# First branch projection of a hybrid decoder layer as four more pairs of seven products, with its token sums made in the mixer

## The chip, the cores and the metric

One core of one Trainium2 chip. The time is that of the device for one execution of the program, in microseconds (us); the median of several runs counts. TensorE (PE) does the matrix products, VectorE (DVE), ScalarE (ACT) and GpSimd (POOL) the elementwise work, SyncE (SP) issues most DMAs. Each engine runs its own instruction stream in order, and the streams meet through semaphores.

## What is computed

One layer of a decoder on 1,024 tokens of width 1,024, float32, from the reference:

```
h = rms_norm(x, norm_w)
proj = einsum('btd,de->bte', h, w_in) + b_in          # 8,720 columns
(a_q, a_k, a_v, a_z, m_q, m_k, m_v, m_i, m_f, m_o, m_z, g_attn, g_mlstm) = split(proj)
attn = sliding_window_sink_attention(a_q, a_k, a_v, sinks)
branch_a = einsum('bte,ed->btd', attn * silu(a_z), w_branch_attn)
h_m = head_rms_norm(mlstm_chunkwise(conv(m_q), conv(m_k), m_v, m_i, m_f))
h_m = sigmoid(m_o) * h_m * silu(m_z)
branch_m = einsum('bte,ed->btd', h_m, w_branch_mlstm)
merged = sigmoid(g_attn) * branch_a + sigmoid(g_mlstm) * branch_m
out = rms_norm(x + einsum('btd,de->bte', merged, w_out), final_norm_w)
```

## The kernel before, in words

**Products.** TensorE multiplies in a format that keeps fewer bits than float32. So each operand is split into a high part (ScalarE, one ACTIVATE Copy) and a low part (full minus high, one TENSOR_TENSOR on VectorE or GpSimd), and a product is the sum of three matmuls: high by high, low tokens by high weights, high tokens by low weights. One matmul takes 128 rows of weights by 512 tokens.

**Pairs.** The input projection is made for two groups of 128 output columns at a time. Such a pair is a 2x2 block product in Strassen's manner: seven products in place of eight, `PRODUCT` = 12 matmuls each (4 slices of 128 features x 3), `PAIR` = 84. The products are called 1, 6, 2, 7, 4, 5, 3, in that order (`ORDER`, L1131), with a bank of PSUM each. Their token operands are seven blocks held in SBUF from the start: `h11`, `s2`, `h12`, `s3`, `h22`, `s1`, `s4`, each a high and a low part of 8 KB per partition, at `H_AT`; three are quarters of the normalised tokens, four are sums of quarters. Their weight operands are four quarters of the pair's weights (`w11`, `w21`, `w12`, `w22`, 256 KB each, loaded by SyncE in `pair_weights`, L617), and three sums made by GpSimd (L818). ScalarE makes the high parts (`high_1` to `high_7`, L1483), GpSimd the low parts (`low`, L820, rows at L823), both in a ring of five slots. VectorE puts the seven banks together (`b_part`, `c11`, `c_part`, `c21`, `c22`, `c12`, L2193 to L2223). A product waits for its weights' low part and for its bank; product 2 of a pair waits for `c12` of the pair before.

**Order of the work.** Turning and norm of the tokens; five dense tiles (k, v, gates); pair 0; four attention steps of three pairs; four mixer steps of five pairs, the last one of four (`WPAIRS` = 32 pairs in all). In an attention or mixer step the small work of the mixer is placed by hand between the matmuls: each of the 8 chunks of a mixer step has two places (`chunk_at`), and on ScalarE and VectorE `retire(position)` (L1783, L2281) does what belongs to the products up to that place. A chunk on TensorE begins with the state products (L1287), which wait for VectorE's state update (L2489 and the operations after it, up to `k_w` at L2517). The gates go to DRAM (`scr_a`, `scr_g`), the attention branch's tokens u to `scr_u`, the mixer's tokens to `scr_m`; those of the last mixer step stay in SBUF (`mz`).

**End of the last mixer step.** TensorE stops 12 matmuls before the end of pair 31, turns the mixer's output (16 transposes, L1315), and does the last 12. Meanwhile SyncE loads u in four blocks of 1 MB over the h blocks as the products of pair 31 end (L670); ScalarE takes a square root with its table load (L1887), then the high parts of u (L1895); VectorE and GpSimd make the low parts.

**Tile stage.** `branch_a_step` (L1362 on TensorE, L1918 on ScalarE, L2566 on VectorE): 8 dense tiles of 48 matmuls (L1344), one per 128 output rows: 8 slices of features x 2 halves of tokens x 3. The weights of a tile (512 KB) are split by GpSimd (`split`, L806 and L808). VectorE multiplies each by its gate into `merged` (L2571) and makes the low parts of the second branch's tokens, held in `UM` at `H_AT` + 64 KB and, for the last two rows, in the mixer's memory (`um_hi67`, `um_lo67`). `branch_m_step` does the same for the second branch and adds (L2619, L2624). Beside it the blocks of the output weights are made: sums s1 to s4 of the quarters (L2596 to L2605), split (L2585), parked in DRAM and loaded back where the memory isn't free yet (`scr_s`, `scr_split`). SyncE's queue is in order: a `wait_ge` in it holds every load behind it.

**End.** Output projection in four pairs of seven products, residual, final norm.

## Time and profile before

| | us |
|---|---|
| median of 3 runs (1077.52 to 1077.68) | 1077.52 |
| the profiled execution | 1077.55 |
| its span | 1075.8 |
| TensorE busy in the span | 1063.5 (99%) |
| VectorE, GpSimd, ScalarE busy | 725.9, 649.7, 516.9 |
| mean granted clock of TensorE, share of full | 0.999 |

The profiled execution is 0.03 us above the median; 1.75 us lie outside its span. A timeline row is start us, us, engine, line, operation, output <- inputs, shape, count, and in brackets the idle time before it and what ended that. Several instructions alike stand in one row ("x2"). Matmuls overlap, so that a matmul's own duration is longer than the distance to the next one.

### The profile page before, as it was taken

To read this page: it belongs to the slowest core of one execution; us is meant where nothing else is said; L and a number is where in the kernel's file an instruction comes from. 1 tells how busy PE (TensorE), PEld (TensorE's weight loads), DVE (VectorE), ACT (ScalarE), POOL (GpSimd) and SP (SyncE) were. 2 spreads that over 40 slices of the span, in tenths; PEclk is the share of its full clock that TensorE was granted. 3 is DMA by queue.
4 is the path that set the end of the run, shared out by engine and by line. 5 is a ranking of instruction groups with operands and counts; after the bars stand their busy time and mean duration, and the time that the engine had idled before them with its cause. 6 is when DMAs were issued, how large, how long until landed. Compare 5 with 4: busy or idle time off the path is not lost.

```text
span 1075.8 us, 18631 instructions
## 1 busy us (share of the span) xinstructions
PE 1063.5 (99%) x6391; PEld 862.7 (80%) x6391; DVE 725.9 (67%) x1144; ACT 516.9 (48%) x1252; POOL 649.7 (60%) x437
## 2 busy tenths in 40 slices
PE   7999999999999999999999999999999999999997
PEld 6887887877877888878888888788788888888886
DVE  5964785776866967566756685669578332558897
ACT  7544755746647643555345444545464311132543
POOL 3577555556555568568955796679654354547441
PEclk9999999999999999999999999999999999999999
DMA  6235132132151231214211431143219434744324
GB/s 220 70 93 89 41 118 80 41 121 76 45 158 40 80 118 40 50 41 147 79 41 50 127 99 39 39 127 88 60 37 363 148 97 151 250 147 164 149 92 143
DMA packets 113851, 111.83 MB, mean 104 GB/s; under 512 B 7340, under 2 KB 96744, under 8 KB 112760
## 3 DMA queue, kind: packets, MB, share of 16 engines
q1 hardware_dynamic: 102648, 77.08, 24.2%
q10 hardware_dynamic: 11136, 33.88, 9.7%
q8 instruction: 39, 0.64, 0.2%
q14 instruction: 28, 0.23, 0.1%
HBM read 84.63 MB, written 26.31 MB: 103 GB/s over the span
## 4 chain that ended last, share of the span: by engine, by line
PE 97%; ACT 1%; DVE 1%; DMA 0%; DVEq 0%; issue 0%; ACTq 0%
PE ps L1066 64%; PE ps L1344 16%; PE ps L973 4%; PE ps L1178 3%; PE ps L1159 2%; PE ps L1233 2%; PE ps L1305 1%; PE ps L1287 1%; PE ps L1302 1%; ACT ev L1441 1%; PE ps L1299 1%; PE ps L1315 1%; PE ps L1253 1%; PE ps L1292 1%; PE ps L1015 1%; ACT h_hi L1450 0%
## 5 line engine op out<-in xcount | busy, mean ns | idle before, releaser
L823 POOL TENSOR_TENSOR ring_lo<-w,ring_hi 128x512 fp32r<-128x512 f32 x128 | 183.1, 1452 | 90.3 <-ACT ring_hi L1483 90.3
L823 POOL TENSOR_TENSOR ring_lo<-t,ring_hi 128x512 fp32r<-128x512 f32 x96 | 132.9, 1389 | 140.1 <-ACT ring_hi L1483 140.1
L1066 PE MATMUL ps<-s_hi,ring_hi 128*128 128x512 f32 x512 | 203.7, 398 | 0.0
L1066 PE MATMUL ps<-s_lo,ring_hi 128*128 128x512 f32 x512 | 200.2, 391 | 0.0
L1066 PE MATMUL ps<-s_hi,ring_lo 128*128 128x512 f32 x512 | 200.1, 391 | 0.0
L1066 PE MATMUL ps<-h_hi,ring_hi 128*128 128x512 f32 x384 | 151.6, 395 | 0.0
L1066 PE MATMUL ps<-h_lo,ring_hi 128*128 128x512 f32 x384 | 150.3, 392 | 0.0
L1066 PE MATMUL ps<-h_hi,ring_lo 128*128 128x512 f32 x384 | 149.9, 390 | 0.0
L1483 ACT ACTIVATE ring_hi<-w 128x512 fp32r<-128x512 f32 x128 | 77.0, 623 | 83.6 <-PE ps L1066 73.5
L1066 PEld LDWEIGHTS ps<-s_hi,ring_hi 128*128 128x128 f32 x512 | 96.2, 188 | 20.9 <-issue 2.5
L1066 PEld LDWEIGHTS ps<-s_hi,ring_lo 128*128 128x128 f32 x512 | 96.2, 188 | 20.0
L1066 PEld LDWEIGHTS ps<-s_lo,ring_hi 128*128 128x128 f32 x512 | 96.3, 188 | 18.4
L818 POOL TENSOR_TENSOR t<-w,t 128x512 f32<-128x512 f32 x64 | 96.8, 1512 | 9.0 <-issue 4.6
L1483 ACT ACTIVATE ring_hi<-t 128x512 fp32r<-128x512 f32 x96 | 59.9, 625 | 73.1 <-PE ps L1066 66.1
L806 POOL TENSOR_TENSOR w_hi<-w_raw,zero_col 128x1024 fp32r<-128x1024 f32 (+1 forms) x18 | 38.3, 2128 | 89.3 <-PE ps L1344 55.7
L1066 PEld LDWEIGHTS ps<-h_hi,ring_hi 128*128 128x128 f32 x384 | 72.3, 188 | 14.8 <-POOL ring_lo L823 0.7
L1066 PEld LDWEIGHTS ps<-h_hi,ring_lo 128*128 128x128 f32 x384 | 72.1, 188 | 14.8
L1066 PEld LDWEIGHTS ps<-h_lo,ring_hi 128*128 128x128 f32 x384 | 72.2, 188 | 13.9
L1344 PE MATMUL ps<-u_a,w_hi 128*128 128x512 f32 x256 | 78.9, 389 | 0.0
L1700 ACT ACTIVATE probs<-probs,neg_max 128x128 f32<-128x128 f32 x128 | 49.7, 390 | 41.3 <-DVE sink_in L2312 41.3
L1914 ACT ACTIVATE ev<-ev 128x1024 f32<-128x1024 f32 x16 | 17.0, 1062 | 107.6 <-DVE merged L2624 48.7
L1344 PE MATMUL ps<-u_m,w_hi 128*128 128x512 f32 x192 | 59.7, 392 | 0.0
(325 smaller groups left out, 2259.9 us busy)
## 6 DMA issues: line engine op xcount, KB each, us to landing
w<-in_w_in SPq DMA_DIRECT2D x128, 256.0 KB, 3.1
xs<-in_x SPq DMA_DIRECT2D x8, 512.0 KB, 7.5
ga_scratch<-ev ACTq DMA_DIRECT2D x4, 1024.0 KB, 4.2
u_scratch<-silu_z ACTq DMA_DIRECT2D x8, 512.0 KB, 3.2
c_rows<-c_scratch ACTq DMA_DIRECT2D x8, 512.0 KB, 6.1
gm_scratch<-ev ACTq DMA_DIRECT2D x4, 1024.0 KB, 5.0
w_raw<-in_w_branch_attn SPq DMA_DIRECT2D x8, 512.0 KB, 4.1
u_a_f<-u_scratch SPq DMA_DIRECT2D x4, 1024.0 KB, 8.4
```

The costliest lines, as they stand in the source:

```text
L806: nc.gpsimd.tensor_tensor(hi, src, zero_col[:].to_broadcast(list(src.shape)), ALU.add)
L818: return nc.gpsimd.tensor_tensor(flat(dst), flat(a), flat(b), op)
L823: return nc.gpsimd.tensor_tensor(flat(lo[:]), flat(raw_or_sum[:]), flat(hi[:]).bitcast(F32), ALU.subtract)
L973: mm = nc.tensor.matmul(ps[:, 2 * s + b, :], w[:, k, :], h[:, k % KH, :], start=(r == 0), stop=(r == KT * TERMS - 1))
L1066: mm = nc.tensor.matmul(ps[:, bank, columns], w[:, k, :], h[:, k, columns], start=(m == 0), stop=(m == PRODUCT - 1))
L1159: mm = nc.tensor.matmul(ps[64 * half:64 * half + 64, SCORES[r], column:column + keys], q_T[rows, j, queries], k_now[rows, first:first + keys],
L1178: mm = nc.tensor.matmul(pv_ps(slice(64 * r, 64 * r + 64), half), v_m, pT[rows, 2 * r:2 * r + 2, queries], start=start, stop=stop)
L1233: mm = nc.tensor.transpose(ps[:, TURNED, h * P:(h + 1) * P], probs[n % 2][:, h, :], ident[:])
L1344: mm = nc.tensor.matmul(ps[:, 2 * s + b, :], w[:, k, :], part(k)[(0, 1, 0)[term]][:, token_half(b)], start=starts, stop=stops)
L1483: return A(ring_slot[0][:], raw_or_sum[:], ACT.Copy)
L1700: A(pr[:, h, :], pr[:, h, :], ACT.Exp, scale=HD ** -0.5, bias=neg_max[:, h:h + 1], accum_out=row_sum[:, h:h + 1])
L1914: A(ev[:, j, :], ev[:, j, :], ACT.Tanh, scale=0.5).then_inc(gate_tanh, 1)
```

## The change

The 8 tiles of the first branch become four more pairs (`BPAIRS`, numbers 32 to 35) of the same seven products; pair `a` gives the output rows `ROWS_OF[a]`. As each product of pair 31 ends, a block of u (or of its sums) is loaded over the h block that it read, ScalarE makes its high part and VectorE its low part; TensorE waits for them in pair 32. The four sums of u are made by VectorE in the middle of each mixer step in `ev`, from rows of u loaded back, and parked in `scr_us`. Turning, norm and gating of the last mixer step are moved into pairs 32 and 33; its tokens now go through `scr_m` too. The second branch's tokens lie where the first's did, and take over the handover that the first had. The making of the output weights' blocks beside the second branch is put in another order, and two blocks instead of one are parked as high and low parts. The diff, cut to its core (`SPAIRS` replaces `WPAIRS` in the output projection and some semaphores are merged; that is left out):

```diff
+BPAIRS = KT // 2
+SPAIRS = WPAIRS + BPAIRS
+ROWS_OF = ((3, 4), (1, 2), (0, 5), (6, 7))
...
-        UA = at("u_a", H_AT, [P, 4, 2, 2, T], F32R)
-        UM = at("u_m", H_AT + 64 * KB, [P, 3, 2, 2, T], F32R)
+        UM = at("u_m", H_AT, [P, 4, 2, 2, T], F32R)
+        BLOCKS = (h11, s2, h12, s3, h22, s1, s4)
+        u_raw = [h_full(f"u_raw{n}", n, 1) for n in range(7)]
...
 SyncE, mlstm_weights(p), after three pairs' weights:
+                sp.wait_ge(m_v_turned, 2 * (p + 1))
+                for j in range(2):
+                    sp.dma_start(ev[:, j, :], scr_u[ds(p + KH * j, 1)]...).then_inc(us_in, 16)
...
 SyncE, after the mixer:
-            first_branch_weights(BA)
-            sp.wait_ge(p1_done, WPAIRS)
-            u_block(0, scr_u, UA_f[:, 0, 1], ua_in[0])
...
+            def branch_weights(a, src=wba_cols):
+                n1, n2 = ROWS_OF[a]
+                pair_weights(WPAIRS + a, n1 * P, n2 * P, src=src)
...
             sp.wait_ge(p1_done, WPAIRS)
+            tokens_block(0)
+            branch_weights(0)
+            sp.wait_ge(us_out, 16 * PAIRS)
+            for n, done in ((1, p6_done), (2, p2_done), (3, p7_done), (4, p4_done), (5, p5_done), (6, p3_done)):
+                sp.wait_ge(done, WPAIRS)
+                tokens_block(n)
+            for a in range(1, BPAIRS):
+                branch_weights(a)
+            sp.wait_ge(mu_out, 16 * PAIRS)
+            sp.wait_ge(w3_ready, SPAIRS)
+            second_branch_weights(BM)
+            for n, done in enumerate((p1_done, p6_done, p2_done, p7_done)):
+                sp.wait_ge(done, SPAIRS)
+                u_block(n)
+            second_branch_weights(BM + 1)
...
+            for i in range(1, KT // 2):
                 weights(BM + 2 * i, [(0, wbm_cols, 2 * P * i)])
                 if i == 1:
                     output_weights([(1, f_o22), (1, f_o12)])
+                if i == 3:
+                    sp.wait_ge(wo_sum, 4)
+                    sp.dma_start(scr_s[1], f_s4[:]).then_inc(wo_stored, 16)
+                    sp.wait_ge(wo_sum, 5)
+                    for part, src in enumerate((part_hi, s3_lo)):
+                        sp.dma_start(scr_split[1, part], src[:].bitcast(F32)).then_inc(wo_stored, 16)
                 weights(BM + 2 * i, [(1, wbm_cols, P + 2 * P * i)])
-                if i == 2:
+                if i == 1:
                     sp.wait_ge(wo_sum, 1)
                     sp.dma_start(scr_s[0], f_s1[:]).then_inc(wo_stored, 16)
                     sp.wait_ge(wo_sum, 3)
-                    sp.dma_start(scr_split[1], s3_lo[:].bitcast(F32)).then_inc(wo_stored, 16)
+                    for part, src in enumerate((part_hi, o22_lo)):
+                        sp.dma_start(scr_split[0, part], src[:].bitcast(F32)).then_inc(wo_stored, 16)
...
 TensorE:
+            def pairs(i0, lo, hi, thirds=False, blocks=None):
                 for q in range(lo // PRODUCT, (hi + PRODUCT - 1) // PRODUCT):
                     a, b = max(lo - q * PRODUCT, 0), min(hi - q * PRODUCT, PRODUCT)
+                    if blocks is not None:
+                        pe.wait_ge(blocks, q + 1)
...
-                more(count * PAIR - (12 if last else 14))
+                if not last:
+                    more(count * PAIR - 14)
+                    turn_h(p)
+                more(count * PAIR)
...
+            for a in range(BPAIRS):
+                if a == 0:
+                    pairs(WPAIRS, 0, PAIR, blocks=u_split)
+                elif a == 1:
+                    pairs(WPAIRS + 1, 0, 3 * PRODUCT)
+                    turn_h(PAIRS - 1)
+                    pairs(WPAIRS + 1, 3 * PRODUCT, PAIR)
+                else:
+                    pairs(WPAIRS + a, 0, PAIR)
...
-            looped(pe, KT // 2, branch_a_step)
...
 ScalarE, mixer step (us_chunk = 4 if last else 3):
+                        act.wait_ge(us_out, 16 * (p + 1))
+                    after(q, i0 + 3, ev_part(0, 0))
+                    if last and q:
+                        block_high(q - 1)
...
+                    if c == us_chunk:
+                        act.wait_ge(us_made, p + 1)
+                        act.dma_start(scr_us[:, :, ds(p, 1)]..., ev[:]...).then_inc(us_out, 16)
...
+            def block_high(n):
+                act.wait_ge(u_in[n], 16)
+                A(BLOCKS[n][0][:], u_raw[n][:], ACT.Copy).then_inc(u_hi, 1)
...
 ScalarE, pairs 32 to 35:
+                    after(q, i, a_part(a)(0, 0), last)
+                    if q == 0 and a == 0:
+                        block_high(6)
+                        store_gm(PAIRS - 1)
...
 VectorE, mixer step (us_chunk = 3 if last else 2):
+                def branch_sums():
+                    dve.wait_ge(us_in, 32 * (p + 1))
+                    dve.sem_inc(passed, 1)
+                    a11, a21, a12, a22 = [ev[:, j, token_half(h)] for j in range(2) for h in range(2)]
+                    V.tensor_tensor(a22, a21, a22, ALU.add)
+                    V.tensor_tensor(a21, a11, a21, ALU.subtract)
+                    dve.drain()
+                    V.tensor_tensor(a11, a22, a11, ALU.subtract)
+                    dve.drain()
+                    V.tensor_tensor(a12, a12, a11, ALU.subtract).then_inc(us_made, 1)
...
+                    if c == us_chunk:
+                        branch_sums()
                     if c < NB:
                         retire(chunk_at(count, c, 1))
...
+                    after(q, i0 + 3, (R_GM + 2 * p, R_GM + 2 * p + 1), ev_part)
+                    if last and 2 <= q <= 4:
+                        block_low(q - 2)
+                    if last and q == 6:
+                        block_low(3)
...
+            def block_low(n):
+                dve.wait_ge(u_hi, n + 1)
+                for part in (slice(0, KH - 1), slice(KH - 1, KH)) if n == 6 else (slice(0, KH),):
+                    V.tensor_tensor(BLOCKS[n][1][:, part, :], u_raw[n][:, part, :], BLOCKS[n][0][:, part, :].bitcast(F32),
+                                    ALU.subtract).then_inc(u_split, 1)
...
 VectorE, pairs 32 to 35:
+            for a in range(BPAIRS):
+                for q in range(7):
+                    after(q, i, (None, None), a_part(a))
+                    if a == 0:
+                        block_low(4), (5), (6) at q == 0, 1, 2; gated_z at q == 4, 5; normalised_h at q == 6
+                    elif q in (1, 2):
+                        gated_a(a - 1, q - 1)
+                    if a == 1 and q == 4:
+                        gated_h(PAIRS - 1)
+                    if last and q in (4, 5):
+                        low parts of the second branch's tokens (second_low)
...
 VectorE, second branch, tile n:
+                if n == 1: wo_in >= 64; f_s1, f_s3 (wo_sum 1, 2); f_s2
+                if n == 2: low part of o22 (wo_sum 3)
+                if n == 4: f_s4 (wo_sum 4)
+                if n == 5: low part of s3 (wo_sum 5)
```

Eight lines of this diff (from "block_low(4)" on, and the last ones) put several of the kernel's lines in words. Every merging operation of a branch pair is that of a projection pair without a bias.

## Rows read from the trace of the kernel before

**Rows 1.** The page, parts 1 and 4: busy time, and the chain that ended last.

```profile
PE 1063.5 (99%) x6391; PEld 862.7 (80%) x6391; DVE 725.9 (67%) x1144; ACT 516.9 (48%) x1252; POOL 649.7 (60%) x437
...
PE 97%; ACT 1%; DVE 1%; DMA 0%; DVEq 0%; issue 0%; ACTq 0%
```

**Rows 2.** The chain that ended last, in order of time: start us, us, what.

```profile
722.30 25.06 PE ps L1066 x110
...
813.20 1.75 PE ps L1315 x16
814.95 2.77 PE ps L1066 x12
817.71 153.30 PE ps L1344 x672
```

**Rows 3.** Timeline of VectorE in the tile stage: start us, us, instruction, idle before.

```profile
883.28 1.22 DVE L2571 SCALAR_TENSOR_TENSOR merged<-ev,ps 128x1024 f32 x1 [7.97 <-PE ps L1344]
...
894.13 1.22 DVE L2571 SCALAR_TENSOR_TENSOR merged<-ev,ps 128x1024 f32<-128x1024 f32 x1 [7.93 <-PE ps L1344]
...
927.02 1.22 DVE L2619 SCALAR_TENSOR_TENSOR ev<-ev,ps 128x1024 f32<-128x1024 f32 x1 [8.49 <-PE ps L1344]
...
934.47 2.29 DVE L2598 TENSOR_TENSOR f_s<-f_o,f_o 128x2048 f32<-128x2048 f32 x1
938.05 1.22 DVE L2619 SCALAR_TENSOR_TENSOR ev<-ev,ps 128x1024 f32<-128x1024 f32 x1 [1.28 <-PE ps L1344]
```

**Rows 4.** Timeline, last mixer step, chunk 3: VectorE, GpSimd, TensorE.

```profile
772.89 0.73 DVE L2223 SCALAR_TENSOR_TENSOR mz<-ps,par,mz 128x512 f32<-128x512 f32 x1
...
777.65 0.47 DVE L2517 TENSOR_SCALAR k_w<-ps,tok_gate 128x64 f32<-128x64 f32 x2
...
772.62 2.54 POOL L823 TENSOR_TENSOR ring_lo<-w,ring_hi 128x512 fp32r<-128x512 f32 x2 [1.74 <-ACT ring_hi L1483]
...
777.41 0.39 PE L1066 MATMUL ps<-h_hi,ring_hi 128*128 128x512 f32 x1
779.54 0.45 PE L1287 MATMUL ps<-state,mq_T 64*64 64x129 f32 x8
```

**Rows 5.** Timeline around 975 us: VectorE, then GpSimd.

```profile
974.00 7.79 DVE L2585 TENSOR_TENSOR o_lo<-f_o,o_hi 128x2048 fp32r<-128x2048 f32 x2
...
973.14 3.20 POOL L808 TENSOR_TENSOR w_lo<-w_raw,w_hi 128x1024 fp32r<-128x1024 f32 x1
976.29 3.36 POOL L904 TENSOR_TENSOR o_t<-merged 128x512 f32<-128x512 f32 x1
```

**Rows 6.** Groups by line: the weights' low parts on GpSimd, all of them.

```profile
L823 POOL TENSOR_TENSOR ring_lo<-w,ring_hi 128x512 fp32r<-128x512 f32 x128 | 183.1, 1452 | 90.3 <-ACT ring_hi L1483 90.3
```

**Rows 7.** Timeline at the end of the last mixer step: SyncE's queue, ScalarE.

```profile
803.11 5.05 SPq L670 DMA_DIRECT2D u_a_f<-u_scratch  x4
...
804.76 1.28 ACT L1887 ACT_TABLE_LOAD   x1
...
809.05 2.01 ACT L1895 ACTIVATE u_a<-u_a_f 128x1024 fp32r<-128x1024 f32 x2 [1.15 <-DMA u_a_f<-u_scratch]
814.18 2.01 ACT L1895 ACTIVATE u_a<-u_a_f 128x1024 fp32r<-128x1024 f32 x2 [0.55 <-DMA u_a_f<-u_scratch]
```

**Rows 8.** Windows: busy us of each engine, granted clock, DMA share, GB/s.

```profile
775.00:778.00 3.00, 3.00 (x17) 2.55 (x16) 2.35 (x8) 2.60 (x10) 1.66 (x2) 1.00 0.71 175
808.00:810.00 2.00, 2.00 (x10) 1.65 (x10) 1.82 (x4) 0.95 (x1) 1.96 (x1) 1.00 1.02 406
1074.00:1075.00 1.00, 0.00 (x0) 0.00 (x0) 0.00 (x0) 0.00 (x0) 0.00 (x0) 0.50 0.84 275
```

**Rows 9.** Tile stage: GpSimd, then a DMA group (KB, us to landing).

```profile
963.72 2.87 POOL L806 TENSOR_TENSOR w_hi<-w_raw,zero_col 128x1024 fp32r<-128x1024 f32 x1 [9.43 <-DMA w_raw<-in_w_branch_mlstm]
966.74 4.26 POOL L808 TENSOR_TENSOR w_lo<-w_raw,w_hi 128x1024 fp32r<-128x1024 f32 x1
...
s_split_scratch<-s_lo SPq DMA_DIRECT2D x1, 1024.0 KB, 5.2
```

528 lines of the change are left out of this document (261 added, 267 removed).

## The prediction

> **What bounds the kernel now.** First the page's busy line and the chain that ended last: TensorE is busy 1063.5 of 1075.8 us and makes 97% of the chain [rows 1]. Then the chain in order of time: 110 matmuls in 25.06 us, the 12 of the last product in 2.77, and 672 of the tile stage in one unbroken piece of 153.30 [rows 2]. So a removed matmul is a gain at its pitch and a wait of TensorE is a loss at its length, and the other engines count only where they come late. The question is where the new order makes them late: a product has its operands ready, or not, at one moment, so I followed each changed stretch in the timelines.
>
> **Matmuls: the gain.** Eight tiles of 48 are 384 matmuls, four pairs of 84 are 336. The pitch is 25.06 / 110 = 0.228 us in the mixer [rows 2], and a tile of the first branch takes 894.13 - 883.28 = 10.85 us, or 0.226 per matmul [rows 3]. I take 0.227: 48 fewer give -10.9. A tile of the second branch takes 938.05 - 927.02 = 11.03 [rows 3], 0.18 more than one of the first though the counts are equal; operands and addresses differ. The second branch's tokens now lie where the first's did. If the address is the cause, 8 x 0.18 = -1.5 more. I take it; the bound is 0. Together -12.4 (bounds -10.9, -12.4). The 16 transposes of 1.75 us [rows 2] move from pair 31 into pair 33: 0 for TensorE, but each product of the end of pair 31 stays where it was and its last one ends 1.75 earlier, at 817.55 - 1.75 = 815.8 (817.55 being 814.95 + 2.77 less the overlap of the last matmul, 0.17).
>
> **The sums in the mixer (A).** Four VectorE operations of 512 columns, each two SBUF inputs, by the 2.29 of one of 2048 [rows 3] 0.6 each and some 0.1 for each drain: 2.85 alone. They wait for two loads of 512 KB, behind which the fourth pair's weights stand in SyncE's queue; at the 2.56 us per MB found below these loads delay those weights by under 3 us, and weights are loaded some products ahead: 0. By `chunk_at` the chunks of steps 0 to 2 are 30 matmuls apart (6.8 us, and the chunk's own small products), which leaves the 2.85 room: 0 there, and 1 each if it doesn't. In the last step they are 18.75 matmuls (4.3 us) apart, and the sums stand ahead of the `c12` of pair 29 (the 0.73 at 772.89), beside two low parts on GpSimd that began at 772.62 and take 2.54 [rows 4]. What two such engines do to each other is seen at 974 us: VectorE's two operations of 2048 take 7.79 where one alone takes 2.29 [rows 3, 5], while GpSimd, whose operations of 512 take 1.27 [rows 4], needs 3.36 for one at 976.29 [rows 5]. Each waits for the other's whole instruction. By this the four sums and GpSimd's two operations alternate, and the sums end at 777.95 in place of 772.9, `c12` at 778.65. Product 2 of pair 30, at 777.41 now, waits for it: 1.25. The state's operations follow five microseconds late as well: `k_w` ends 778.12 [rows 4] + 5.2 = 783.3, and the state product that starts at 779.54 [rows 4] + 1.25 = 780.8 waits 2.5 more. A = 3.7. Without the exclusion the sums end near 775.8 and `k_w` at 778.12 + 2.85 = 781.0: +1.5. Bounds 0 and 4.5.
>
> **The handover in pair 31 (B).** Before, u lands in four blocks issued from 803.11 on; the high parts start at 809.05 and 814.18, two blocks apart, so 5.13 / 2 = 2.56 us per MB; the DMA moves 406 GB/s then [rows 7, 8]. A block's high part is 2.01 us of ScalarE. Now SyncE issues block 0, the four weights of pair 32 and blocks 1 to 6, each block as its product of pair 31 ends. A product takes 12 x 0.227 = 2.72, so product 1 ends six of these before 815.8, at 799.4. Weights move at 175 GB/s in 0.71 of the DMA's time [rows 8], 247 GB/s, so 1.06 us for each 256 KB. I estimate 1.8 us from a product's end to the first byte and 0.6 from the last to the semaphore: block 0 is there at 799.4 + 1.8 + 2.56 + 0.6 = 804.4, and as the queue then never runs dry, the last weights at 804.4 + 4 x 1.06 = 808.6, blocks 1 to 6 2.56 apart at 811.2, 813.8, 816.4, 818.9, 821.5, 824.0. ScalarE: high part of block 1 811.2 to 813.1, the square root with its table load of 1.28 [rows 7] to 814.6, block 2 to 816.5, and only then the high part of `w11` for pair 32, at 817.0, since each block's high part stands ahead of the next weights'. VectorE takes block 2's low part at 816.5 (2.28 for 2048 columns, by [rows 3]), GpSimd's low part of `w11` waits for it to 818.7 and is done at 820.0. TensorE wants product 1 at 815.8: **a stall of 4.2**. Nothing covers it, as every product of pair 31 is done.
>
> What is late next: block 3's low part ends 823.4, GpSimd's sum 824.7, block 4's low part 826.9, `w21` 828.1, where product 2 wants it at 820.0 + 2 x 2.72 = 825.4: +2.7. By the same alternation product 7 is 0.7 late, product 4 1.4, and product 2 of pair 33 +2.2, behind the moved norm of the mixer's output on VectorE. B = 4.2 + 2.7 + 0.7 + 1.4 + 2.2 = 11.2. Without exclusion the high part at 817.0 and GpSimd's 1.27, and 0.1 for the semaphore, still give 818.4, +2.6, and the rest vanishes. Bounds 2.6 and 13.
>
> That exclusion is what decides, and another row speaks against it: GpSimd's 128 low parts of weights have a mean of 1452 ns [rows 6], only 14% over 1.27, though VectorE is busy two thirds of the time. I explain it by VectorE's usual merges, which read one operand from PSUM. The Trainium skill has a rule on this ("SBUF — State Buffer", section "Who interferes with whom"): a VectorE instruction with two SBUF inputs contends with a GpSimd instruction that reads SBUF, and the one that is second is fully blocked until the first is done; every added VectorE operation here is of that kind. The trace agrees at 974 us, and the rule speaks against this change; by the mean alone the whole sum would be that of the first rival.
>
> The clock: after TensorE's last work the granted clock falls to 0.50 at 1074 to 1075 [rows 8], half of full, 1.2 GHz; in the stages here it is 1.00. A stall of 4.2 could be long enough to lose it for a while. A product of 2.72 would then take 5.4, but the 2.7 after it is a wait that it would fill: 0 taken, bound +3. The Trainium skill says the same of an idle engine ("TensorE: Matmul & The Clock Gate", Part 1); no row here shows a stall of this length inside the work.
>
> **The other parts.** The second handover, pair 35 to the second branch, is the old one with the same four blocks and the same order: 0. Gating in SBUF, two operations of 1024 per pair, lies in VectorE's free time under the 19 us of a pair: 0. The second branch (C): o22's low part is made after the second tile, behind two tiles and their gating, at about T0 + 25 (T0: start of the branch), and beside a split on GpSimd, by 7.79 / 2 rather than 2.29 and with the sums still queued before it; I get 30.6 for its end. SyncE's two stores of 1 MB (5.2 us to land for one [rows 9]; 2.56 each in a row) then stand ahead of the weights of the fifth tile, which land at 30.6 + 1.8 + 5.1 + 1.5 + 0.6 = T0 + 39.6. GpSimd's split is 2.87 and 2 x 1.27 less some overlap, or 4.26 where it met VectorE [rows 9]: 44.7, against four tiles of 10.85, 43.4. C = +1.3 (bounds 0, 5). Before, the weights of the last tile already arrive just in time: a split that waited for its DMA ends at 971.0 [rows 9].
>
> **Sum.** -12.4 + 3.7 + 11.2 + 1.3 = +3.8: 1077.55 + 3.8 = 1081.3 us. The profiled execution stands 0.03 above the median of the runs, so that is the forecast for both.
>
> **Rivals.**
> 1. *The waits are short* (faster). GpSimd and VectorE overlap as the mean says [rows 6]: A 1.5, B 2.6, C 0.3, sum -8.0: 1069.5. For it: the mean, and that only `w11` is then late. Against: 7.79 for two operations. Chance 0.27.
> 2. *Half-way* (no change, or slightly faster). Product 1 waits its 4.2, but later products are in time, as the block loads or GpSimd's sums come 1 to 2 us earlier than my schedule; A 2, B 8, C 1: -1.4, 1076.2. Chance 0.20; within 0.2% 0.15, faster 0.05.
> 3. *No stall*: blocks and sums in time everywhere: 1065.1. It needs `w11` split before 815.8, so its high part ahead of block 2's, which the order on ScalarE excludes unless block 2 lands 2 us early. Chance 0.08.
> 4. My forecast, slower: ScalarE's order holds `w11` back and the port alternates. Chance 0.45. It decides slower from 12.4 us of added waits on.
>
> **Numbers.** A measurement of this kernel can tell some 0.2%, 2.15 us, from no change. Faster: 0.27 + 0.08 + 0.05 = 0.40; same 0.15; slower 0.45. The likeliest case has its own range, from 1079.7, the edge of no change, to 1086 (A 4.5, B 13, C 2.5: +7.6, and a little for the clock). The range reaches down to 1068, past rival 1 and short of rival 3; above 1086 lies 0.05.
>
> **What would show it.** Right: TensorE idle about 4 us before the first matmul of pair 32, ended by GpSimd's low part, whose start is VectorE's low part's end; further gaps before products 2, 7 and 4; a gap at chunk 3 of the last mixer step; blocks' low parts far over 2.29 or GpSimd's far over 1.27. Wrong: gaps that add up to under 10 us, or a TensorE that ends pair 31 later than 815.8 + 3.6. The tile pitch of the second branch shows the 0.18 right if it falls from 11.03 to 10.85.

## The result and the profile after

The changed kernel takes 1095.09 us (median of 4 runs, 1092.65 to 1095.91) against 1077.58 before (1077.52 to 1077.68): a ratio of 1.0159, 95% interval 1.0145 to 1.0174. It is slower, by over four times the 3.8 us forecast, and lies above the range. The four runs of before lie within 0.16 us of each other, those of the changed kernel within 3.3. The profiled execution took 1094.62, its span is 17.1 us longer.

The page of the changed kernel, against [rows 1]: first the span, then the busy line, then the chain that ended last.

```profile
span 1092.9 us, 18700 instructions
...
PE 1060.9 (97%) x6343; PEld 858.0 (79%) x6343; DVE 777.1 (71%) x1188; ACT 538.4 (49%) x1283; POOL 683.4 (63%) x465
...
PE 81%; DVE 5%; DMA 5%; POOL 4%; ACT 2%; issue 1%; DVEq 1%; POOLq 1%; ACTq 0%; SPq 0%
```

TensorE's busy time fell by 2.6 us only, though 48 matmuls are gone (some ran at half the clock and so count longer), and its share of the chain fell from 97 to 81%: it now waits. Every wait of over 0.5 us from the last mixer step on is in the timeline of TensorE. The bracket is the idle time before the instruction and what ended it:

```profile
778.21 0.47 PE L1077 MATMUL ps<-h_hi,ring_hi 128*128 128x512 f32 x1 [0.91 <-DVE mz L2250]
...
782.34 0.45 PE L1304 MATMUL ps<-state,mq_T 64*64 64x129 f32 x8 [1.81 <-DVE k_w L2576]
...
822.89 0.47 PE L1077 MATMUL ps<-h_hi,ring_hi 128*128 128x512 f32 x1 [4.17 <-POOL ring_lo L834]
...
830.74 0.46 PE L1077 MATMUL ps<-h_hi,ring_hi 128*128 128x512 f32 x1 [0.53 <-issue]
...
838.02 0.47 PE L1077 MATMUL ps<-h_hi,ring_hi 128*128 128x512 f32 x1 [1.56 <-issue]
...
852.96 0.50 PE L1077 MATMUL ps<-h_hi,ring_hi 128*128 128x512 f32 x1 [1.04 <-POOL ring_lo L834]
...
910.56 0.50 PE L1381 MATMUL ps<-u_m,w_hi 128*128 128x512 f32 x1 [1.11 <-ACT u_m L1975]
...
958.20 1.21 PE L1381 MATMUL ps<-u_m,w_hi 128*128 128x512 f32 x2 [6.04 <-POOL w_lo L819]
...
995.21 0.73 PE L1381 MATMUL ps<-u_m,w_hi 128*128 128x512 f32 x2 [1.56 <-POOL w_lo L819]
...
1024.91 0.64 PE L1077 MATMUL ps<-o_s_hi,o_ring_hi 128*128 128x512 f32 x1 [1.90 <-DVE o_s_lo L2674]
```

These ten sum to 20.6 us. The brackets count from the end that the profile gives the matmul before; measured from start to start, less one step, a wait is 0.1 to 0.4 longer. By starts, TensorE's work divides like this; "own" is the count of matmuls by 0.2267 us, the step from one to the next where nothing waits, and 1.67 for the transposes:

| stretch of the changed kernel | us | own | lost | forecast |
|---|---|---|---|---|
| last mixer step: pair 31 ends 818.56, without loss 815.56 | | | 3.0 | 3.7 (A) |
| to the second branch, 906.57 (pairs 32 to 35) | 88.0 | 77.8 | 10.2 | 11.2 (B) |
| second branch, to 1006.23 | 99.7 | 87.1 | 12.6 | 1.3 (C) |
| output projection and end, 82.6 before | 86.7 | 82.6 | 4.1 | 0 |

The losses are 29.9. Against them stand 12.8 us gained: before, the end of pair 31 to the end of the second branch took 175.7 us, the same now without its losses 164.9; 1.75 of transposes are gone from pair 31 (their 1.67 is in the 164.9); 0.24 is an earlier start of the last mixer step (its first piece in the chain starts at 722.06, 722.30 in [rows 2]). 29.9 - 12.8 = 17.1.

The clock, which the forecast had put at nothing, is in these losses. Windows of the changed kernel (length, busy us of PE, PEld, DVE, ACT, POOL, then the granted clock, DMA share, GB/s):

```profile
820.00:822.00 2.00, 0.00 (x0) 0.00 (x0) 2.00 (x2) 2.00 (x2) 2.00 (x1) 1.00 1.06 388
...
824.00:826.00 2.00, 2.00 (x6) 1.52 (x5) 2.00 (x1) 2.00 (x4) 2.00 (x2) 0.50 1.05 388
...
958.00:960.00 2.00, 1.80 (x4) 1.49 (x5) 2.00 (x1) 0.00 (x0) 2.00 (x2) 0.50 0.62 207
...
1026.00:1028.00 2.00, 2.00 (x6) 1.52 (x6) 1.93 (x4) 0.00 (x0) 0.00 (x0) 0.50 0.00 0
```

After the idle stretches at 820, 953 and 1023 the granted clock is 0.50, the lower level of 1.2 GHz, and the matmuls step by 0.43 us in place of 0.23. Eight steps are hit after the first, 1.6 us, twelve after the second, eight after the third, 1.6 again. The tile after the second idle stretch takes 13.53 us by starts against 10.88 for its neighbours: 2.6 us more.

**The last mixer step (A)** on VectorE, three of the four sums and the delayed `c12` (it was at 772.89 in [rows 4]), then GpSimd:

```profile
772.69 1.50 DVE L2529 TENSOR_TENSOR ev<-ev 128x512 f32<-128x512 f32 x1
774.11 1.75 DVE L2530 TENSOR_TENSOR ev<-ev 128x512 f32<-128x512 f32 x1
775.94 0.69 DVE L2532 TENSOR_TENSOR ev<-ev 128x512 f32<-128x512 f32 x1
...
777.32 0.74 DVE L2250 SCALAR_TENSOR_TENSOR mz<-ps,par,mz 128x512 f32<-128x512 f32 x1
...
772.35 2.97 POOL L834 TENSOR_TENSOR ring_lo<-w,ring_hi 128x512 fp32r<-128x512 f32 x2 [1.74 <-ACT ring_hi L1513]
```

A sum of 512 takes 1.5 and 1.75 us beside GpSimd's two low parts, 0.69 once they are done at 775.3: the alternation. `c12` starts 4.4 us late.

**The handover (B)**, ScalarE, VectorE, GpSimd in turn:

```profile
814.08 1.92 ACT L1927 ACTIVATE s_hi<-u_raw 128x2048 fp32r<-128x2048 f32 x1 [4.65 <-DMA u_raw<-u_sums_scratch]
...
817.43 1.90 ACT L1927 ACTIVATE h_hi<-u_raw 128x2048 fp32r<-128x2048 f32 x1
...
819.24 0.61 ACT L1513 ACTIVATE ring_hi<-w 128x512 fp32r<-128x512 f32 x1
```

```profile
819.37 2.29 DVE L2629 TENSOR_TENSOR h_lo<-u_raw,h_hi 128x2048 fp32r<-128x2048 f32 x1 [0.38 <-ACT h_hi L1927]
```

```profile
819.92 2.87 POOL L834 TENSOR_TENSOR ring_lo<-w,ring_hi 128x512 fp32r<-128x512 f32 x1 [4.30 <-ACT ring_hi L1513]
...
827.30 7.88 POOL L834 TENSOR_TENSOR ring_lo<-w,ring_hi 128x512 fp32r<-128x512 f32 x3
```

Block 1 lands at 814.0; the forecast's 811.2 and the 3.0 of A make 814.2. Block 2's high part stands ahead of w11's, which ends at 819.85. GpSimd starts at 819.92, VectorE is in block 2's low part until 821.6, and GpSimd ends at 822.79: 2.87 us, of which 1.27 are its own and 1.6 the wait for VectorE. TensorE starts pair 32 at 822.89. Then three low parts take 7.88 us in place of 3.8 (three of 1.27).

**The second branch (C)**. VectorE, SyncE's queue, GpSimd:

```profile
905.43 9.10 DVE L2643 TENSOR_TENSOR u_m<-u_m_f,u_m 128x1024 fp32r<-128x1024 f32 x6
...
915.22 2.87 DVE L2638 SCALAR_TENSOR_TENSOR merged<-ev,merged 128x1024 f32<-128x1024 f32 x1
925.58 1.22 DVE L2708 SCALAR_TENSOR_TENSOR ev<-ev,ps 128x1024 f32<-128x1024 f32 x1 [6.36 <-ACT ev L1939]
...
928.03 2.29 DVE L2685 TENSOR_TENSOR f_s<-f_o,f_o 128x2048 f32<-128x2048 f32 x1
...
939.70 2.28 DVE L2674 TENSOR_TENSOR o_lo<-f_o,part_hi 128x2048 fp32r<-128x2048 f32 x1
```

```profile
942.01 0.34 SPq L740 DMA_DIRECT2D s_split_scratch<-part_hi  x1
...
943.16 1.16 SPq L713 DMA_DIRECT2D w_raw<-in_w_branch_mlstm  x1
```

```profile
952.89 1.89 POOL L817 TENSOR_TENSOR w_hi<-w_raw,zero_col 128x1024 fp32r<-128x1024 f32 x1 [14.20 <-DMA w_raw<-in_w_branch_mlstm]
```

The first tile's gating starts at 925.58. If the gating followed each tile at once, as the forecast took it, it would be at 917.5, one tile of 10.88 after 906.57; the tile ends at 919.36, since the handover costs it 1.9, and VectorE is 6.2 later still. VectorE was in the low parts of the second branch's tokens until 914.5 and then in the last pair's gating, whose first operation ends at 918.1; only after that can the first gate row be loaded into `ev` (issued 918.12, landed 924.5). The sums for the output weights follow at 928, o22's low part ends at 942.0, and SyncE, which waited for it, issues the two stores and then the fifth tile's weights at 943.16. They land at 952.8. GpSimd's split then takes until 958.1.

**The output projection**: the last block's load in the chain, issued when the last tile is done, with 5 MB ahead of it:

```profile
1006.42 13.22 DMA f_again<-s_scratch
```

### The profile page after: what moved, and what is told of

It is laid out like the page before. It is cut to its first block, busy times and chain, and to the rows that moved or that the text cites. A ratio compares the mean times of both kernels' runs of the same rounds, so it can differ in the third digit from the quotient of the medians.

```text
span 1092.9 us, 18700 instructions
## 1 busy us (share of the span) xinstructions
PE 1060.9 (97%) x6343; PEld 858.0 (79%) x6343; DVE 777.1 (71%) x1188; ACT 538.4 (49%) x1283; POOL 683.4 (63%) x465
## 4 chain that ended last, share of the span: by engine, by line
PE 81%; DVE 5%; DMA 5%; POOL 4%; ACT 2%; issue 1%; DVEq 1%; POOLq 1%; ACTq 0%; SPq 0%
PE ps L1077 62%; PE ps L984 4%; PE ps L1195 3%; POOL ring_lo L834 2%; PE ps L1381 2%; PE ps L1176 2%; PE ps L1250 2%; DMA w_raw<-in_w_branch_mlstm 2%; DMA f_again<-s_scratch 1%; PE ps L1322 1%; PE ps L1304 1%; DMA u_raw<-u_sums_scratch 1%; DVE u_m L2643 1%; ACT ev L1471 1%; PE ps L1319 1%
## 5 line engine op out<-in xcount | busy, mean ns | idle before, releaser
L834 POOL TENSOR_TENSOR ring_lo<-w,ring_hi 128x512 fp32r<-128x512 f32 x144 | 212.9, 1499 | 93.1 <-ACT ring_hi L1513 93.1
L834 POOL TENSOR_TENSOR ring_lo<-t,ring_hi 128x512 fp32r<-128x512 f32 x108 | 152.9, 1420 | 146.7 <-ACT ring_hi L1513 146.7
L1077 PE MATMUL ps<-s_hi,ring_hi 128*128 128x512 f32 x576 | 228.6, 397 | 0.0
L1077 PE MATMUL ps<-s_lo,ring_hi 128*128 128x512 f32 x576 | 225.1, 391 | 0.0
L1077 PE MATMUL ps<-s_hi,ring_lo 128*128 128x512 f32 x576 | 225.0, 391 | 0.0
L1077 PE MATMUL ps<-h_hi,ring_hi 128*128 128x512 f32 x432 | 171.6, 397 | 8.2 <-POOL ring_lo L834 5.2
L1077 PE MATMUL ps<-h_lo,ring_hi 128*128 128x512 f32 x432 | 169.7, 393 | 0.0
L1381 PE MATMUL ps<-u_m,w_hi 128*128 128x512 f32 x256 | 81.1, 399 | 8.9 <-POOL w_lo L819 7.6
L829 POOL TENSOR_TENSOR t<-w,w 128x512 f32<-128x512 f32 x36 | 56.3, 1565 | 16.5 <-issue 9.2
L1381 PEld LDWEIGHTS ps<-u_m,w_hi 128*128 128x128 f32 x256 | 49.2, 193 | 20.8 <-issue 6.5
```

What stands on the lines that cost most here:

```text
L829: return nc.gpsimd.tensor_tensor(flat(dst), flat(a), flat(b), op)
L834: return nc.gpsimd.tensor_tensor(flat(lo[:]), flat(raw_or_sum[:]), flat(hi[:]).bitcast(F32), ALU.subtract)
L1077: mm = nc.tensor.matmul(ps[:, bank, columns], w[:, k, :], h[:, k, columns], start=(m == 0), stop=(m == PRODUCT - 1))
L1381: mm = nc.tensor.matmul(ps[:, 2 * s + b, :], w[:, k, :], part(k)[(0, 1, 0)[term]][:, token_half(b)], start=starts, stop=stops)
```

## The experiments

Run 1, `e1_sums_later`: the last step's sums behind `c12`.

```diff
-                    if c == us_chunk:
+                    if c == us_chunk and not last:
                         branch_sums()
...
                             silu_z_part(z_chunks.index(c))
                             dve.drain()
+                        if c == us_chunk and last:
+                            branch_sums()
```

> In the last mixer step the four token-sum operations stand behind the merge c12 of pair 29 and the chunk's silu part instead of ahead of them; all else is the changed kernel. Theory (the sums delay the state's operations, step A): the two gaps of TensorE near 778 and 782 us, 0.91 and 1.81 in the record and 3.2 us by the starts of the matmuls, fall to under 1, and the time falls by 2 to 3 us. Rival (the gaps come from the two 512 KB loads that delay pair 30's weights): the gaps stay and the time is the same.

1097.13 (1094.67 to 1099.91). The wait for `c12` is gone, the other is larger by more:

```profile
782.68 0.45 PE L1304 MATMUL ps<-state,mq_T 64*64 64x129 f32 x8 [3.19 <-DVE k_w L2576]
```

3.19 in place of 0.91 + 1.81, and the granted clock falls behind it, which the changed kernel's did not: pair 31 ends 1.95 us later, 1.6 of it by the clock. A miss: the place within the chunk does not matter, since the state's operations come after either. It does not tell the operations from the loads yet.

Run 2, `e2_weights_first`: SyncE's queue alone.

```diff
+                if i == 2:
+                    sp.wait_ge(wo_sum, 3)
+                    for part, src in enumerate((part_hi, o22_lo)):
+                        sp.dma_start(scr_split[0, part], src[:].bitcast(F32)).then_inc(wo_stored, 16)
+                weights(BM + 2 * i, [(1, wbm_cols, P + 2 * P * i)])
                 if i == 3:
                     sp.wait_ge(wo_sum, 4)
...
-                weights(BM + 2 * i, [(1, wbm_cols, P + 2 * P * i)])
                 if i == 1:
                     sp.wait_ge(wo_sum, 1)
                     sp.dma_start(scr_s[0], f_s1[:]).then_inc(wo_stored, 16)
-                    sp.wait_ge(wo_sum, 3)
-                    for part, src in enumerate((part_hi, o22_lo)):
-                        sp.dma_start(scr_split[0, part], src[:].bitcast(F32)).then_inc(wo_stored, 16)
```

> In SyncE's queue the weights of the fifth tile of the second branch go ahead of the two stores of o22's parts and of the wait for VectorE's third sum, the weights of the eighth ahead of the three stores of s4 and s3; nothing else is moved. Theory (a wait in the queue holds the weights): the stalls of 6.0 and 1.6 us before tiles 5 and 8 vanish, and with the first the 2.8 us that tile 5 runs slow behind it (13.70 against 10.9): 9 to 10 us less. Rival (the DMA is full, or GpSimd's split is held by VectorE): the weights land as late as before and under 3 us are gained. The stall of 1.9 in the output projection stays or grows, as the stores come later.

1080.01 (1079.06 to 1083.33), ratio to before 1.0030 (1.0020 to 1.0041). The two stalls and the slow tile are gone, 15.1 us by the medians (13.6 between the profiled executions) rather than 10, as the wait in the output projection falls too, from 1.90 to 0.73, and with it the clock's fall there. The rows show two tiles' gating, 963.30 and 974.18:

```profile
963.30 1.22 DVE L2709 SCALAR_TENSOR_TENSOR ev<-ev,ps 128x1024 f32<-128x1024 f32 x1 [4.44 <-PE ps L1382]
...
974.18 1.22 DVE L2709 SCALAR_TENSOR_TENSOR ev<-ev,ps 128x1024 f32<-128x1024 f32 x1 [3.52 <-PE ps L1382]
```

10.88 us per tile, against 11.03 in [rows 3]: 0.15 less. That is the whole difference: by the starts of its matmuls a tile of the first branch took 10.88 before too, and the 10.85 that the forecast read from two gatings was 0.03 short. No run moved the tokens alone, so that their address is the cause is not shown.

Run 3, `e3_low_quarters`: each block's low part in four operations of 512.

```diff
-                for part in (slice(0, KH - 1), slice(KH - 1, KH)) if n == 6 else (slice(0, KH),):
-                    V.tensor_tensor(...).then_inc(u_split, 1)
+                for k in range(KH):
+                    part = slice(k, k + 1)
+                    ins = V.tensor_tensor(...)
+                    if k == KH - 1 or (n == 6 and k == KH - 2):
+                        ins.then_inc(u_split, 1)
```

> Each low part of a token block on VectorE is made in four operations of 512 columns instead of one of 2048. Theory (VectorE with two SBUF inputs and GpSimd exclude each other for a whole instruction): GpSimd's low part of w11, 2.87 us in the changed kernel of which 1.27 is its own, falls to under 2, and the stall before pair 32 from 4.2 to about 3; the later stalls shrink too; 1.5 to 4 us less. Rival (no exclusion, the lateness is ScalarE's and the loads'): the stall stays at 4.2 and the time is the same or, by the fixed cost of 21 more operations, up to 1 us longer.

1098.98 (1097.45 to 1099.80). The first stall falls by 1.1 us, GpSimd's low part of w11 takes 1.26 in place of 2.87, as the exclusion has it; the time does not follow:

```profile
821.79 0.76 PE L1077 MATMUL ps<-h_hi,ring_hi 128*128 128x512 f32 x1 [3.10 <-POOL ring_lo L834]
...
838.31 0.50 PE L1077 MATMUL ps<-h_hi,ring_hi 128*128 128x512 f32 x1 [3.70 <-DVE h_lo L2630]
```

4.17 became 3.10, but now VectorE's blocks are late, 3.70 before product 4. From the last matmul of pair 31 to the first of the second branch it is 89.4 us by starts (818.30 to 907.74), 88.2 in the changed kernel. The rest of the 4 us is in longer stalls before the fifth and the eighth tile, 8.9 and 3.7. They differed between the four profiles with the change's queue (6.0 to 8.9 and 1.6 to 3.7), and the first of them fits the exclusion too: where it was 8.9 (runs 1 and 3), VectorE's second sum for the output weights took 3.98 us in place of 2.28, and GpSimd's low part for the fifth tile 4.2 in place of 3.15.

Run 4, `e4_high_first`: block 2 and the later ones one step back on ScalarE.

```diff
-                    if last and q:
-                        block_high(q - 1)
+                    if last and q in (1, 2):
+                        block_high(q - 1)
+                    if last and q >= 4:
+                        block_high(q - 2)
...
                     if q == 0 and a == 0:
+                        block_high(5)
                         block_high(6)
```

> On ScalarE the high parts of token blocks 2 to 6 are each made one product later, so that the high part of w11 for pair 32 stands ahead of block 2's. Theory (ScalarE's order holds w11 back): w11's high part starts near 817.5 instead of 819.2, GpSimd is not blocked by block 2's low part, and the stall before pair 32 falls from 4.2 to 1 to 1.5 us, with it most of the 1.9 us at the halved clock; blocks 5 and 6 come later and may cost 1 to 2 back before products 5 and 3; 3 to 5 us less in all. Rival (the loads of the blocks are what is late, 814.1 for block 1 where 811.2 was forecast): the stall moves to product 6 or 2 and the time falls by under 1 us.

1095.96 (1094.12 to 1097.55). The stall is where it was forecast to be, at 1.1, and comes back elsewhere:

```profile
821.81 0.47 PE L1077 MATMUL ps<-h_hi,ring_hi 128*128 128x512 f32 x1 [1.13 <-POOL ring_lo L834]
...
825.83 0.47 PE L1077 MATMUL ps<-s_hi,ring_hi 128*128 128x512 f32 x1 [1.02 <-DVE ev L2253]
...
830.20 0.47 PE L1077 MATMUL ps<-h_hi,ring_hi 128*128 128x512 f32 x1 [1.39 <-issue]
...
839.54 0.47 PE L1077 MATMUL ps<-h_hi,ring_hi 128*128 128x512 f32 x1 [3.04 <-issue]
```

By starts it is 87.8 (820.29 to 908.13): 0.4 better, not 3. Here pair 31 ended 2.0 later, 1.6 of it because the clock fell after the wait of the sums, before any edit has its effect; it had not done so in the changed kernel's profile. The window of this run, granted clock 0.50:

```profile
784.00:786.00 2.00, 2.00 (x8) 1.71 (x8) 1.13 (x3) 1.21 (x4) 1.57 (x2) 0.50 0.00 0
```

The same wait of 1.8 us costs the clock in one execution and not in another. How much of the spread of 3 us between executions comes from this is not shown, as only one execution of each kernel has a trace.

Runs 5 to 8 stand on run 2. Run 5, `e5_no_last_sums`, leaves out the last step's sums.

```diff
+                    if last:
+                        V.tensor_tensor(a12[:, 0:8], a12[:, 0:8], a11[:, 0:8], ALU.subtract).then_inc(us_made, 1)
+                        return
```

> On the kernel with the weights first in SyncE's queue (e2_weights_first, 1080.01). Left out: the token sums of the last mixer step (one operation of 8 columns stands for the four of 512), so the blocks of the last two rows of u's sums hold the plain rows. Theory (the four operations themselves delay the state's chain): both gaps near 778 and 782 us go, and pair 31 ends 3.2 us earlier; 1076.8, if the handover that follows is not bound by the loads. Rival (the two loads before the sums do it): the gaps stay and the time stays at 1080.

1076.67 (1076.04 to 1078.58): 3.3 less, no gap there, pair 31 ends 2.9 earlier than in run 2. The operations cost it; the loads before them are still there and cost nothing.

Run 6, `e6_filled`: matmuls in the stall.

```diff
+                    pe.wait_ge(u_split, 1)
+                    until(pe, c21_out, WPAIRS)
+                    for m in range(14):
+                        nc.tensor.matmul(ps[:, product_bank(0, None), :], h11[0][:, m % KH, 0:P], h11[0][:, m % KH, :],
+                                         start=True, stop=True)
                     pairs(WPAIRS, 0, PAIR, blocks=u_split)
```

> On e2_weights_first. 14 matmuls of 128x512 on block 0, 3.2 us of work whose result is thrown away, stand on TensorE ahead of its wait for the weights of pair 32, in the bank that product 1 then overwrites; they are done inside the stall of 4.2 to 4.7. Theory (the halved clock after the stall is a cost of its own, 8 matmuls at 0.43 in place of 0.23): the granted clock stays at 1.00 from 820 to 830, product 1 starts as late as before, and 1.5 to 2 us are gained. Rival (the following products wait for GpSimd anyway, so that the time lost at the low clock is hidden behind the next stall): the clock stays up but the gap before product 2 grows by the same 1.9, and the time is the same. If the clock falls all the same, both are wrong.

1081.35 (1079.71 to 1082.20), no gain. The windows show the clock held at 1.00 over the first stretch and lost in the second; the row after them is product 2:

```profile
818.00:828.00 10.00, 9.56 (x41) 7.18 (x40) 9.53 (x7) 10.00 (x12) 8.45 (x4) 1.00 0.99 357
...
828.00:840.00 12.00, 9.86 (x36) 7.81 (x36) 9.30 (x7) 2.41 (x2) 11.71 (x6) 0.86 0.70 215
```

```profile
830.37 0.47 PE L1078 MATMUL ps<-h_hi,ring_hi 128*128 128x512 f32 x1 [2.15 <-issue]
```

The rival is right, with 1.6 us for its 1.9: the wait before product 2 grew from 0.5 to 2.15, and after that the clock fell. What the low clock lost in pair 32 was hidden behind the next wait. Run 11 shows it once more, with no fall of the clock at all.

Run 7, `e7_no_low_parts`: no low parts of the blocks.

```diff
-                    V.tensor_tensor(BLOCKS[n][1][:, part, :], u_raw[n][:, part, :], ..., ALU.subtract).then_inc(u_split, 1)
+                    V.memset(BLOCKS[n][1][:, part, :].bitcast(F32), 0.0).then_inc(u_split, 1)
```

> On e2_weights_first. Left out: the low parts of the seven token blocks; a memset of the same memory, which reads nothing from SBUF, stands for each subtraction. Theory (VectorE's two-input subtractions hold GpSimd's low parts of the weights back, step B): GpSimd's operations of pair 32 take 1.3 us each where they took up to 3.4, the stall before pair 32 falls to about 3 (ScalarE's order is left as it was) and the later ones in pair 32 (0.5 and 1.6) vanish; 3 to 4 us less. Rival (ScalarE's order or the loads are the limit throughout): stalls and time as before.

1074.07 (1073.06 to 1077.61): 5.9 less. GpSimd's low part of w11, then the three after it:

```profile
820.35 1.27 POOL L835 TENSOR_TENSOR ring_lo<-w,ring_hi 128x512 fp32r<-128x512 f32 x1 [5.85 <-ACT ring_hi L1514]
...
825.17 3.80 POOL L835 TENSOR_TENSOR ring_lo<-w,ring_hi 128x512 fp32r<-128x512 f32 x3
```

and TensorE's first matmul of pair 32:

```profile
821.72 0.77 PE L1078 MATMUL ps<-h_hi,ring_hi 128*128 128x512 f32 x1 [3.00 <-POOL ring_lo L835]
```

1.27 against 2.87, and 3.80 against 7.88. After the one stall of 3.0, pairs 32 and 33 have no gap. The stretch by starts is 82.9 (818.33 to 901.25), in run 2 it is 88.7 (818.22 to 906.95). This memset takes 1.76 us where the subtraction takes 2.29, so VectorE is not idle in its place; it just does not hold GpSimd. The exclusion is shown by GpSimd's durations. Its price is not quite the 5.9 us, since each block's operation is also 0.5 shorter on VectorE. That ScalarE's order has the 3.0 that remain fits run 4, where w11's high part went first and the wait was 1.1.

Run 8, `e8_sums_spread`: one sum per chunk.

```diff
...
+                    if last and c in (2, 3, 4, 5):
+                        branch_sum_of(c - 2)
-                    if c == us_chunk:
+                    if c == us_chunk and not last:
                         branch_sums()
...
-                us_chunk = 4 if last else 3
+                us_chunk = 6 if last else 3
```

> On e2_weights_first. The last mixer step's four token sums are spread over chunks 2 to 5, one behind each chunk's state operations, with the store two chunks later; nothing is left out. Theory (a chunk of the last step has room for under 1 us on VectorE's chain, not for the 2.85 of all four): gaps near 778 and 782 us fall from 2.75 in the record to under 1 in sum, 2 to 3 us less, about 1077.5. Rival (any added operation on the chain costs its length, as the run with the sums moved behind c12 suggests, whose gap was 3.2): the gaps only spread over four chunks and the time stays at 1080.

1077.16 (1076.40 to 1078.08), ratio to before 0.9997 (0.9987 to 1.0006): 2.9 less, both gaps gone, with all four operations done. So a chunk has room for one of them.

Run 9, `e9_fifth_only`, is the changed kernel with the first of run 2's two moves.

> On the changed kernel: only the fifth tile's weights go ahead of the two stores of o22's parts; the eighth's stay behind the stores of s4 and s3, as in the change. Theory (each wait in the queue has its own price, and the loss before tile 5 is 6 to 9 of stall and 2 to 3 of halved clock): the stall before tile 5 and the slow tile vanish, the one before tile 8 stays at 1.6 to 3.7, and so does the late last load of the output blocks; 1084 to 1087. Rival (the stall before tile 5 hides one that follows, so that tile 8 waits longer): over 1088.

1085.34 (1083.83 to 1088.70). Before the eighth tile, and in the output projection:

```profile
986.35 0.74 PE L1382 MATMUL ps<-u_m,w_hi 128*128 128x512 f32 x2 [1.56 <-POOL w_lo L820]
...
1016.08 0.47 PE L1078 MATMUL ps<-o_s_hi,o_ring_hi 128*128 128x512 f32 x1 [2.06 <-DVE o_s_lo L2675]
```

So the fifth tile's place in the queue is 9.8 us of the 15, the eighth's the other 5.3, with what it costs in the output projection, where TensorE waits 2.06 and in run 2 only 0.73.

Run 10, `e10_norm_later`, and run 11, `e11_spread_high_first` (the edit of run 4), stand on run 8.

```diff
-                        if q == 6:
-                            normalised_h(PAIRS - 1)
...
-                    if a == 1 and q == 4:
-                        gated_h(PAIRS - 1)
+                    if a == 1 and q == 2:
+                        normalised_h(PAIRS - 1)
+                    if a == 1 and q == 6:
+                        gated_h(PAIRS - 1)
...
-                    pairs(WPAIRS + 1, 0, 3 * PRODUCT)
+                    pairs(WPAIRS + 1, 0, 5 * PRODUCT)
                     turn_h(PAIRS - 1)
-                    pairs(WPAIRS + 1, 3 * PRODUCT, PAIR)
+                    pairs(WPAIRS + 1, 5 * PRODUCT, PAIR)
```

> On e8_sums_spread (1077.16). The norm of the last mixer step's output on VectorE (2048 elements, 2.2 us alone, 3.3 beside GpSimd) comes four products later, its transposes stand before product 5 of pair 33 instead of before product 7, its gating two products later. Theory (GpSimd's low part of w21 for pair 33 waits for that operation): the 1.0 to 1.2 us stall before product 2 of pair 33 vanishes, and nothing new comes; 1076.0. Rival (GpSimd is behind anyway by what it lost in pair 32): the stall stays or moves to product 7 and the time is 1077.2.

1076.67 (1075.65 to 1079.83). The gap in pair 33 is gone and the stretch by starts is 87.1 after 88.4 (815.34 to 902.44, 815.33 to 903.73), as the theory has it, but the medians differ by 0.5 with overlapping runs: unclear by the time alone.

> On e8_sums_spread (1077.16), ScalarE's order of e4_high_first: w11's high part ahead of block 2's. Theory as it stands after seven runs (from the end of pair 31 to product 7 of pair 33 the pace is set by the sum of VectorE's and GpSimd's operations, which exclude each other; the order only says where TensorE waits): the stall before pair 32 falls from 4.3 to about 1, the others grow by as much, that stretch stays at 38.5 to 39 us, and the time is within 1 us of 1077.2. Rival (the stall before pair 32 and the halved clock behind it are a loss of their own): 1073 to 1075.

1076.71 (1075.60 to 1078.53). The first wait is 0.85, the next ones 1.05, 1.38, 0.30, 3.03, 1.01: 7.6 us in other places, and the clock stays at 1.00 in these pairs. In run 8 they are 4.33, 1.56 and 1.03, 6.9 in all, and the halved clock behind the first. The stretch by starts is 87.5 (815.40 to 902.91) after 88.4, but the second handover takes 0.5 of that back, and the median is 0.45 less with overlapping runs: no gain clear of noise.

Run 12, `e12_idle_order`, on run 10.

```diff
-                    if last and q:
-                        block_high(q - 1)
+                    if last and q == 1:
+                        block_high(0)
+                    if last and q >= 4:
+                        block_high(q - 3)
...
                     if q == 0 and a == 0:
+                        block_high(4)
+                        block_high(5)
                         block_high(6)
```

> On e10_norm_later (1076.67). ScalarE's order at the handover again: the square root with its table load comes right after block 0's high part instead of after block 1's, w11's high part before block 1's, the sum t2's before block 2's, blocks 3 and 4 one step later. GpSimd then makes the low part of w11 while VectorE and GpSimd both stand idle in front of block 1 (3.7 us of it in the changed kernel), instead of in the stretch in which they exclude each other. Theory (the stretch lasts as long as the sum of their operations from block 1's landing on): 1.3 us of GpSimd's leave the stretch, 1.5 of ScalarE's too, and 1.5 to 3 us are gained: 1074 to 1075. Rival (only the stretch's end counts, set by the last blocks' landing or by VectorE alone): 1076.7 as before.

1075.33 (1074.94 to 1077.94), ratio to before 0.9984 (0.9974 to 0.9993). GpSimd's low part of w11, and the two larger waits of TensorE that are left in pair 32:

```profile
812.50 1.29 POOL L835 TENSOR_TENSOR ring_lo<-w,ring_hi 128x512 fp32r<-128x512 f32 x1
```

```profile
816.75 0.47 PE L1078 MATMUL ps<-h_hi,ring_hi 128*128 128x512 f32 x1 [1.20 <-DVE ev L2255]
...
831.60 0.47 PE L1078 MATMUL ps<-h_hi,ring_hi 128*128 128x512 f32 x1 [2.55 <-issue]
```

It now runs at 812.50, in 1.29 us, and block 1's low part starts on VectorE at 812.94. The stretch is 86.5 (815.16 to 901.66), in run 10 it is 87.1. The medians differ by 1.3, of the 1.5 to 3 expected, and the two sets of runs overlap. This is the fastest version here that leaves nothing out: 2.0 us under the kernel before and 19.8 under the changed one.

## Why the prediction was wrong

The direction, slower, and both mechanisms named for it hold. The size fails, and by one step first. Of the 17.5 us measured, 15.1 go with the order of SyncE's queue (run 2), which the forecast had at 1.3; with that put right, A and B against the gain leave 2.5.

- **The step that failed: "C = +1.3 (bounds 0, 5)", and in it the end of o22's low part, forecast at T0 + 30.6.** It ended at T0 + 35.4 (906.57 to 942.0) and the weights landed 10.8 us behind that in place of 9.0, at T0 + 46.2, not T0 + 39.6. The wait of SyncE on `wo_sum` was seen and priced, but VectorE's start was taken as if it came free with the branch. It did not: low parts, the last pair's gating, and then a gate row that can only be loaded once `ev` is free came first, and with the late first tile they put the first gating 8.1 us behind the forecast. The stall was 6.0 where 1.3 was forecast, and 2.6 more at the half clock.
- **The same queue, once more.** The eighth tile's weights stand behind three stores and `wo_sum` 5, and 5 MB of loads stand ahead of the last block; the sum had no term for either. The wait is 1.6, and 4.1 were lost in the output projection, 1.6 of them by the clock. Run 9 against run 2 prices them together at 5.3.
- **The second handover** was forecast as the old one, at 0. It costs 1.9 by starts (1.11 and 0.21 by the brackets), as ScalarE still waits for the last blocks of tokens to land (2.49 and 1.08 us) when TensorE wants their high parts.
- **The clock, "0 taken".** It fell after three stalls. In pair 32 it cost nothing that could be measured, as the forecast argued and runs 6 and 11 show. In the second branch nothing waited behind it to hide it, and it cost 2.6, in the output projection 1.6.
- **A and B were right** in mechanism and near in size. A: 3.7 forecast, 3.0 by starts and 3.3 by run 5. B: 11.2 forecast, 10.2 measured; the stall before pair 32 was forecast at 4.2 and is 4.17; with A's 3.0 added, the forecast's times for the landing of block 1, the start and the end of w11's low part are each within some 0.2 us of the trace. The later waits come where they were forecast but are smaller: before product 2 0.5 (2.7 forecast, of which the 1.6 at the half clock took the place), before product 4 1.6 (1.4), before product 2 of pair 33 1.0 (2.2), and before product 7 none (0.7). That B's sum comes within 1.0 is in part luck. The mean of GpSimd's low parts, which spoke for the first rival, was no guide: 1452 ns before, and the rule of the rows at 974 us held (run 7). The Trainium skill's rule ("SBUF — State Buffer", section "Who interferes with whom"), that the second of the two is blocked in full until the first is done, agrees with the trace: 2.87 us for an operation of 1.27 that met the last 1.6 us of VectorE's.
- **The gain** was 12.4 forecast and 12.8 measured, of which 0.24 is the earlier start of the last mixer step.
- With the queue's order put right (run 2) the kernel takes 1080.01, where the forecast of 1081.3 had A, B and almost no C.

The rivals: "the waits are short" and "no stall" are refuted by the waits of the changed kernel, and runs 5 and 7 show what they come from. "Half-way" is not what happened, and the time of run 8 is near it for another reason: A is gone.

What stays open: whether pairs 32 and 33 are held by the sum of VectorE's and GpSimd's operations alone. Runs 3, 4, 6 and 11 say that order does little (87.5 to 89.4 by starts, where kernels with the old order have 88.2 to 88.8), run 7 that removing the exclusion does much (82.9). In run 12, which takes one operation out of the stretch, it is 86.5 after run 10's 87.1: 0.6, no more than what separates two orders, so that it doesn't settle the question. Fewer operations there with the same exclusion were not tried beyond that.

## What to carry to other kernels

A store that waits for a slow engine must not stand ahead of a load that TensorE needs. Price such a queue by the earliest time at which that engine is really free, with what the stage before has left on it, and not from the start of the stage. Where VectorE and GpSimd both read two operands from SBUF, add their times as if they were one engine, as a first estimate: from 819.4 to 839.6 in the changed kernel, 20.3 us, VectorE's five low parts of 2.29 and GpSimd's eight operations of 1.27 make 21.6. There, changing the order mostly moved the waits; taking work out of the stretch, into a moment when both stand idle, gave the fastest version here, by a small margin. On a kernel whose TensorE never waits, a stall can cost some time again in clock (1.6 us behind one of 1.9, 2.6 behind one of 6.0), unless another wait follows.

## What was not expected of the hardware

- **A wait of under 2 us can cost the clock, and the same wait may not.** The wait for `k_w` (1.8 us, in front of the 8 small state products) left the clock at 1.00 in the changed kernel and took it to 0.50 for 784 to 786 us and 0.74 after in run 4, whose code is the same up to there. A wait of 2.06 us in the output projection left it at 1.00 in run 9, one of 1.90 there took it in the changed kernel. In pair 32 a wait of 3.0 left it in runs 4 and 11, and one of 2.55 took it in run 12. What tells these cases apart is not shown. After the waits of 3.9 to 4.7 us before pair 32 it fell in every profile, unless the stall was filled (run 6). The Trainium skill ("TensorE: Matmul & The Clock Gate", Part 1) describes a clock that falls to half after idleness; these runs agree with the two levels, 1.00 and 0.50.
- **VectorE's operation of 2048 takes 2.29 us when it comes first and up to 3.4 when GpSimd is in the way**, and GpSimd's three of 512 took 7.88 between VectorE's, 3.80 beside memsets (run 7). The single waits that can be read in the rows fit whole operations of the other engine: 2.87 is 1.27 and the 1.6 that were left of VectorE's.
